# Squares summed while attention runs, a later first weight load, router logits in column groups, the second gate applied on GpSimd, and one block for experts, spare blocks and final sums

## What is computed

```
mods = split(silu(cond) @ w_ada + b, 6)              # shift/scale/gate 1, shift/scale/gate 2
h1   = modulate(rmsnorm(x), shift1, scale1)
f, q, k, v = split(h1 @ w_in)
fout = real(fft2(f, 64 channels x positions)) @ w_fmix
nout = neighbourhood_attention(q, k, v, k_ctx, v_ctx, rpb)   # 12 heads, 8x16 window + 256 context keys
x1   = x + gate1 * (concat(rmsnorm(fout), rmsnorm(nout)) @ w_out)
h2   = modulate(rmsnorm(x1), shift2, scale2)
lg, le = h2 @ w_rg, h2 @ w_re                        # 4 group logits, 32 expert logits
group = argmax(lg);  two experts of the 8 in it;  gate = softmax weight * group probability
y    = sum over the 2 experts of gate * (silu(h2 @ w_gate[e]) * (h2 @ w_up[e])) @ w_down[e]
x2   = x1 + gate2 * y
out  = rmsnorm(x2, g_final)
```

## Time and profile before

| | |
|---|---|
| runs | 1292.05, 1292.8, 1293.32 us, median 1292.8 |
| profiled execution | 1292.83 us, span 1291.0 us |
| busy | PE 1232.0 us (95%), DVE 934.3 (72%), ACT 706.7 (55%), POOL 249.9 (19%) |
| mean granted TensorE clock | 0.981 |
| first tiles | 0 to 34 us |
| projection, attention | 34 to 333, 333 to 518 us |
| mixing, choice and lists | 519 to 640, 640 to 657 us |
| experts | 657 to 1245 us, 17.76 us each |
| finish | 1245 to 1291 us |

### The profile page before, as it was taken

The page is one execution under the profiler, slowest core; times in us unless marked ns, Lnnn a source line. Parts: engine busy times, 40 slices in busy tenths (PEclk is TensorE's granted clock), DMA queues, the critical chain, the costliest instruction groups (busy, mean ns, idle before and its releaser), DMA issues. The chain is left out here.

```text
span 1291.0 us, 18692 instructions
## 1 busy us (share of the span) xinstructions
PE 1232.0 (95%) x7306; PEld 1024.4 (79%) x7306; DVE 934.3 (72%) x1105; ACT 706.7 (55%) x827; POOL 249.9 (19%) x201
## 2 busy tenths in 40 slices
PE   4799999999999999999989999999999999999966
PEld 1799888888788888888878888888888888888852
DVE  2656544332688887556669998989989888989847
ACT  3832212112556665322247777878787877778723
POOL 0000000001101000000011542623535265321001
PEclk8899999999999999999899999999999999999988
DMA  9648844434577772600559999999999999999756
GB/s 379 239 181 295 283 149 157 159 114 164 201 234 160 170 181 81 235 36 34 180 198 354 383 392 390 374 392 376 384 384 377 393 377 390 380 383 386 252 195 262
DMA packets 94459, 343.81 MB, mean 266 GB/s; under 512 B 17387, under 2 KB 45731, under 8 KB 66723
## 3 DMA queue, kind: packets, MB, share of 16 engines
q1 hardware_dynamic: 74499, 311.37, 65.8%
q10 hardware_dynamic: 10656, 14.43, 3.8%
q0 software_dynamic: 9216, 16.80, 3.5%
HBM read 313.70 MB, written 39.33 MB: 273 GB/s over the span
## 5 line engine op out<-in xcount | busy, mean ns | idle before, releaser
L2010 DVE TENSOR_TENSOR w_low<-raw,w_high 128x2048 fp32r<-128x2048 f32 x128 | 293.4, 2313 | 30.8 <-ACT w_high L1950 28.0
L1950 ACT ACTIVATE w_high<-raw 128x2048 fp32r<-128x2048 f32 x128 | 241.1, 1910 | 9.6 <-DVEq L1312 9.6
L2010 DVE TENSOR_TENSOR w_low<-arena,w_high 128x2048 fp32r<-128x2048 f32 x64 | 146.4, 2290 | 31.6 <-ACT w_high L1950 31.6
L1950 ACT ACTIVATE w_high<-arena 128x2048 fp32r<-128x2048 f32 x64 | 122.1, 1908 | 3.2 <-DMA arena<-in_w_down 3.2
L1909 POOL DMA_INDIRECT y_rows<-arena,row x32 | 48.1, 1504 | 324.2 <-ACT arena L1971 322.6
L1867 PE MATMUL p_g<-w_high,x_high 128*128 128x512 f32 x252 | 101.7, 404 | 2.0 <-DVE w_low L2010 1.1
L1867 PE MATMUL p_u<-w_high,x_high 128*128 128x512 f32 x256 | 102.3, 400 | 0.0
L1867 PE MATMUL p_a<-tokens_high,half_high 128*128 128x512 f32 (+1 forms) x272 | 101.8, 374 | 0.2 <-DVE half_low L698 0.2
L1868 PE MATMUL p_a<-tokens_low,half_high 128*128 128x512 f32 (+1 forms) x272 | 100.9, 371 | 0.0
L1869 PE MATMUL p_a<-tokens_high,half_low 128*128 128x512 f32 (+1 forms) x272 | 100.8, 371 | 0.0
L1869 PE MATMUL p_u<-w_high,x_low 128*128 128x512 f32 x256 | 100.0, 391 | 0.0
(11 more groups left out here) (344 smaller groups left out, 2823.4 us busy)
## 6 DMA issues: line engine op xcount, KB each, us to landing
raw<-in_w_gate SPq DMA_DIRECT2D x64, 1024.0 KB, 8.3
raw<-in_w_up SPq DMA_DIRECT2D x64, 1024.0 KB, 7.9
arena<-in_w_down SPq DMA_DIRECT2D x64, 1024.0 KB, 8.4
raw<-in_w_ada SPq DMA_DIRECT2D x24, 1024.0 KB, 7.8
x<-qk_rows SPq DMA_DIRECT2D x6, 1664.0 KB, 9.0
raw<-in_w_chunks SPq DMA_DIRECT2D x9, 1024.0 KB, 5.8
qk_rows<-x SPq DMA_DIRECT2D x18, 512.0 KB, 2.6
yy<-y_rows SPq DMA_DIRECT2D x8, 1024.0 KB, 13.5
```

The lines of the kernel that those rows point to most:

```text
L1950: act.activation(x.high[i % SPLITS][:], x.raw[j][:, :], ACT.Copy).then_inc(high_ok, 1)
L2010: dve.tensor_tensor(x.low[i % SPLITS][:], x.raw[j][:, :], x.high[i % SPLITS][:], ALU.subtract).then_inc(low_ok, 1)
```

## The change

At the start, the first weights are loaded after all eight pieces of `w_ada` instead of after the sixth; only the first half of them is made high in the first block, and all low parts and the second high part move to the projection's start. In attention, the Fourier squares are summed by PE inside steps 8 to 11, the squares of the last pair of tiles move from ACT to DVE (`add_last`), PE sums `acc` between and after the last steps, the eighteen transposes become 4 and 3, and the first tile's high and low parts (`first_high`, `first_low`) are made in steps 43 and 44. The mixing block starts with products. `route` has the weights stationary (64 columns, 36 of them weights, the rest zeros), two halves of k in two column groups, so that the turned logits are copied by ACT (`move_logits`) and joined by one matmul against `pair` (`join`). The last tile's scaling moves to ACT (`scale_last`) and two POOL multiplications and additions. In the experts POOL multiplies each y by gate2 before it is scattered; the last one is multiplied on DVE from PSUM. The finish is in the same block as the experts, starts when all rows are written, and makes each tile of three steps: DVE adds y0 x gate0 (`begin`), ACT multiplies y1 by gate1, POOL adds. Some semaphores and buffers are renamed or shared.

```diff
@@ first_tiles, SP, ACT and DVE
-                    if k == 5:
-                        load_weights(sp, a, s, 0)
+                load_weights(sp, a, s, 0)
-                for q in range(2):
-                    act.activation(half_chunk(s, s.w_high2, q), raw_half(s, q), ACT.Copy).then_inc(s.half_high, 1)
                 act.wait_ge(multiplied, KD)
                 act.activation(flat[0:64, :], p_r[0:64, :], ACT.Copy)
+                wait_weights(act, s, 0)
+                act.activation(half_chunk(s, s.w_high2, 0), raw_half(s, 0), ACT.Copy).then_inc(s.half_high, 1)
-                for q in range(2):
-                    dve.tensor_tensor(half_chunk(s, s.w_low2, q), raw_half(s, q), half_chunk(s, s.w_high2, q), ALU.subtract)
@@ project, ACT and DVE
+                        if g == 0 and r == 0:
+                            split(1)
-                lows(0)
+                for r in range(2):
+                    split(r)
+                    lows(0, (r,))
@@ attention, PE
+                    if NT <= n < NT + NT // 2:
+                        for i in (2 * (n - NT), 2 * (n - NT) + 1):
+                            pe.matmul(s.group_sums[:, NT + i:NT + i + 1], s.f_squares[:, 0, i * P:(i + 1) * P], s.ones[:, 0:1], start=True, stop=True)
@@ mix_and_route, PE
-                    for k in range(KD):
-                        last = pe.matmul(p_l[:, n * 36:(n + 1) * 36], xt[n % 2][:, k, :], wrs[:, k, :], start=(k == 0), stop=(k == KD - 1))
-                    last.then_inc(logits, 1)
+                    for k in range(KD // 2):
+                        for g in range(2):
+                            last = pe.matmul(p_l[64 * g:64 * g + 64, SUMS:SUMS + P], wrs[:, 4 * g + k, :], xt[n % 2][:, 4 * g + k, :],
+                                             start=(k == 0), stop=(k == KD // 2 - 1))
+                    last.then_inc(routed, 1)
+                def join(n):
+                    pe.wait_ge(moved_l, n + 1)
+                    pe.matmul(p_l[:, n * 36:(n + 1) * 36], turned_logits, pair[:], start=True, stop=True).then_inc(logits, 1)
@@ mix_and_route, last tile: ACT, POOL, DVE
+                def scale_last():
+                    act.activation(xrow[(NT - 1) % 2][:], s.x1[:, NT - 1, :], ACT.Copy, scale=rstd[:, 2, NT - 1:NT]).then_inc(scaled_last, 1)
+                pool.tensor_tensor(last[:], last[:], scale2, ALU.mult).then_inc(scaled_last, 1)
+                pool.tensor_tensor(last[:], last[:], shift2, ALU.add).then_inc(scaled_last, 1)
                 halves = one_e.rearrange("p (k n) -> p k n", k=2)
+                dve.wait_ge(scaled_last, 4)
@@ main_experts, POOL
                 pool.wait_ge(y_ok, n + 1)
+                if n < NE - 1:
+                    pool.tensor_tensor(x.y[b], x.y[b], x.gate2[:], ALU.mult).then_inc(y_scaled, 1)
+                    pool.wait_ge(y_scaled, n + 1)
                 pool.indirect_dma_start(a.y_rows, ...
@@ main_experts, DVE, after the last split
+            dve.tensor_tensor(halves(x.y[(NE - 1) % 2]), x.p_y[:], halves(x.gate2[:]), ALU.mult).then_inc(y_ok, 1)
@@ finish (no block of its own)
+        def add(i):                                   # POOL, tiles 0 to 6
+            pool.tensor_tensor(s.x1[:, i, :], s.x1[:, i, :], yy[i][:, 1, :], ALU.add).then_inc(added, 1)
+        def gate(i):                                  # ACT, tiles 0 to 6
+            act.activation(yy[i][:, 1, :], yy[i][:, 1, :], ACT.Copy, scale=s.gates[:, 1, i:i + 1]).then_inc(gated, 1)
+        def begin(i):                                 # DVE, all tiles
+            dve.scalar_tensor_tensor(s.x1[:, i, :], yy[i][:, 0, :], s.gates[:, 0, i:i + 1], s.x1[:, i, :], ALU.mult, ALU.add).then_inc(begun, 1)
+        def end(i):                                   # DVE, tile 7
+            dve.scalar_tensor_tensor(s.x1[:, i, :], yy[i][:, 1, :], s.gates[:, 1, i:i + 1], s.x1[:, i, :], ALU.mult, ALU.add).then_inc(ended, 1)
-NORMS = [(0, 2), (2, 2), (4, 2), (6, 2)]
+NORMS = [(0, 2), (2, 2), (4, 2), (6, 1), (7, 1)]
```

More of the change, by code:

```diff
@@ L1245, in weigh, with sums @@
                     last.then_inc(weighted, 1)
+                def sums(*tiles):
+                    for i in tiles:
+                        pe.matmul(s.group_sums[:, i:i + 1], s.acc[:, i * P:(i + 1) * P], s.ones[:, 0:1], start=True, stop=True)
                 for n in range(STEPS + 2):
@@ L1502, in move_x @@
                     if n >= 2:
[L1503 removed]
+                        dve.wait_ge(routed, n - 1)
                     dve.tensor_copy(xt[n % 2][:, 4:8, :], p_t[1][:].rearrange("p (k q) -> p k q", k=4)).then_inc(t_dve, 1)
[L1506 removed]
+                group_sums()
+                norm_groups()
                 split(EARLY)
[L1508 to L1511 removed]
+                split(EARLY + 1)
                 scale_f(0)
+                split(EARLY + 2)
                 low_f(0)
+                split(EARLY + 3)
                 low(1)
@@ L1653, in _ @@
                 for n in range(NT):
-                    last = pe.matmul(p_r[:, n:n + 1], s.acc[:, n * P:(n + 1) * P], s.ones[:, 0:1], start=True, stop=True)
-                for n in range(NT):
-                    last = pe.matmul(p_r[:, NT + n:NT + n + 1], s.f_squares[:, 0, n * P:(n + 1) * P], s.ones[:, 0:1], start=True, stop=True)
-                last.then_inc(sums_ok, 1)
-                for n in range(NT):
                     mix_na(n)
+                    if n >= 2:
+                        join(n - 2)
                     if n >= 1:
@@ L1999, in _ @@
             split(NE - 1, 5)
-            move_y(NE - 1)
+            act.wait_ge(over_ready, over.STEPS)
+            spare.scalar(act, spare.count(act))
+            last.scalar(act)
         @block.vector
@@ L2049, in _ @@
             split(NE - 1, 5)
+            dve.wait_ge(c_in, 80)
+            dve.wait_ge(scattered[(NE - 1) % 2], 16 * ((NE - 1) // 2))
+            dve.wait_ge(used, place[NE - 1, 5] + 1)
+            halves = lambda y: y.rearrange("p (c n) -> p c n", c=2)
+            dve.tensor_tensor(halves(x.y[(NE - 1) % 2]), x.p_y[:], halves(x.gate2[:]), ALU.mult).then_inc(y_ok, 1)
+            spare.vector(dve, spare.count(dve))
+            last.vector(dve)
         @block.tensor
@@ new lines, in tensor, with body @@
+    def tensor(pe, count):
+        def body(n):
+            pe.wait_ge(q.gathered[0], (n + NE // 2 + 1) * 16)
+            for k in range(KD):
+                last = pe.transpose(x.p_x[:, k, :], every(x.xg[0], k, KD), s.ident[:])
+            last.then_inc(q.x_turned, 1)
+            pe.wait_ge(q.x_high, n + NE + 1)
+            for j in range(4):
+                pe.wait_ge(q.loaded[j], (n + NE + 1) * 16)
+                for i in range(4):
+                    k = 4 * (j % 2) + i
+                    last = pe.matmul((x.p_g, x.p_u)[j // 2][:], x.x_whole[:, k, :], x.raw[j][:, i * DE:(i + 1) * DE],
+                                     start=(k == 0), stop=(k == KD - 1))
+                if j % 2 == 1:
+                    last.then_inc(q.used, 1)
+            pe.wait_ge(q.h_ok, n + NE + 1)
+            for k in range(KE):
+                last = pe.transpose(x.p_h[:, k, :], every(x.h, k, KE), s.ident[:])
+            last.then_inc(q.h_turned, 1)
+            pe.wait_ge(q.h_high, n + NE + 1)
+            for j in (4, 5):
+                pe.wait_ge(q.loaded[j], (n + NE + 1) * 16)
+                for h in range(2):
+                    for i in range(2):
+                        k = 2 * (j - 4) + i
+                        last = pe.matmul(x.p_y[:, h, :], x.h_whole[:, k, :], x.raw[j][:, i * D + h * 512:i * D + (h + 1) * 512],
+                                         start=(k == 0), stop=(k == KE - 1))
+            last.then_inc(q.used, 1)
+        each(pe, count, body)
```

638 lines of the change are left out of this document (339 added, 299 removed).

## The result

The changed kernel takes 1319.6 us (median of 4 runs, 1315.5 to 1322.8) against 1293.1 before: a ratio of 1.019, 95% interval 1.017 to 1.021. I had forecast 1284.4 and faster.

What follows compares the result with a forecast made beforehand. The prediction took TensorE's own work and its waits as the bound (1232.0 of 1291.0 us busy). Terms −1.4 − 2.1 − 1.4 − 3.2 + 1.0 − 0.35 + 2 − 3 = −8.45 took 1292.83 to 1284.4 us, range 1272 to 1299.

Steps and rivals of the forecast that it cites:

- Experts: Expert loop: GpSimd's gate multiplications cost +2 us, mostly covered by VectorE's spare time, with room in GpSimd's queue.
- The price on **VectorE: Experts: GpSimd's multiplication holds VectorE, which has 1.99 us spare per expert; between nothing and +8.6 us, taken as +2.
- Rival A: Experts: each gate multiplication exceeds VectorE's spare time, so VectorE becomes the bound; 1298.9 us or near 1317; chance 0.21.
- second price: Rival A with each multiplication taking 3.0 us from VectorE: +1.0 us per expert, near 1317 us.
- Choice: Expert choice: last tile's scaling on ScalarE and GpSimd slows VectorE's small operations; +1.0 us, up to +2.9.
- Finish: Final sums: earlier loads, additions shared with GpSimd; −3 us, between −8.5 (no disturbance) and +3 (full turns).
- Router and clock: Mixing: cheaper routes by two overlapping column groups, −3.2 us; no clock fall at the first products, −1.4 us.
- Start: Kernel start: later weight load lets the `w_ada` pieces land 2.5 us earlier, 1.1 taken back; −1.4 us.
- End of attention: Attention to mixing: sums moved into earlier steps and fewer transposes bring mixing's first product earlier; −2.1 us.

Runs made afterwards that it cites:

- no_gate: Changed kernel with GpSimd's 31 gate multiplications left out of the experts: 1291.5 us, ratio 0.998.
- spread: Changed kernel with GpSimd's 80 small table operations issued 3 or 4 at a time in experts 1 to 24 instead of in bunches: 1292.6 us, ratio 0.999.
- places_spread: Changed kernel with only the two bunches of eight 128x128 table operations spread, two in each of experts 17 to 24: 1301.3 us, ratio 1.005.
- spread_finish_dve: The kernel of spread, with VectorE making both sums of every tile in the finish, none on GpSimd, no gate scaling on ScalarE: 1286.0 us, ratio 0.993.
- route_old: Changed kernel with VectorE replacing GpSimd for gate, last tile's scaling and finish sums, plus the earlier kernel's router: 1284.2 us, ratio 0.993.
- start_old: Changed kernel with VectorE replacing GpSimd for gate, last tile's scaling and finish sums, plus the earlier kernel's start: 1283.2 us, ratio 0.992.
- gate_any: Changed kernel multiplying by x1 of tile 0 instead of the gate rows, which are loaded only in the last expert: 1320.1 us, ratio 1.020.
- before_gate: Kernel before the change, plus GpSimd multiplying each of the first 31 results by x1 of tile 0 before its scatter: 1308.2 us, ratio 1.013.

## Why the prediction was wrong

The step that failed is in **Experts**: "POOL is nearly empty ... the queue behind (a gather, needed an expert later) can stand 2.4 us". I read it from GpSimd's 19% of the span and from an expert without tables. In five of the eight experts with a bunch GpSimd was still at work on it, or on the gather behind it, when the next result was ready to be scattered, and the gather behind the bunch landed only 1.4 to 4.3 us before its use. (In the other three it had 3.6 to 5.6 us of rest.) Four of these five gathers are the ones that TensorE waits for in the changed kernel. I had L1825 in the earlier trace rows as evidence on VectorE, with its 4.72 us, and didn't add eight of them up against the next gather. The runs show the size: against no_gate, the same multiplications cost 28 us (changed kernel) or 1.1 (spread), by where the table operations stand. places_spread gives 18 of the 27 us between the changed kernel and spread to the two bunches of L1935. The lower clock behind the late gathers, 4.6 us in the trace, is a term that the prediction's experts did not have at all.

The price on **VectorE** was nearly right. The hold is 2.2 us (I had bounds of 0 and 2.37), that is 0.2 above the 1.99 of spare time, by the prediction's own sum 30 × 0.2 − 2.8, some 3 us, and the stretch of spread is 542.3 against 540.9 before: +1.4 for my +2. Rival A, VectorE as the bound of all experts, happened only with the doubled multiplication. Its second price, near 1317, lies close to the measured 1319.6 by accident: it has every period 1.0 us longer, and 16 of the 31 in the changed kernel are within 0.1 of the 17.76 of before. The Trainium skill (SBUF — State Buffer, section "SBUF: two separate sides") has this as an exclusive lock for a whole instruction; the traces agree, 4.50 for 2.28 beside a multiplication of 2.37, and 6.75 for 2.48 beside two additions. By that page's rule the prediction had +8.6 for this term, where spread shows +1.4, and 1298.9 with the choice and the finish: slower, but for another reason than the one that decided.

**Choice**: right mechanism, mis-sized. The prediction's upper bound was +2.9 and the stage grew by 4.4. Two of VectorE's small operations lost 3.7 us, and the traces with and without GpSimd's two operations are 3.6 apart on average.

**Finish**: I took the middle between no collision (−8.5) and full turns (+3), reasoning that the scalings fall where GpSimd is free (the terms of the −8.5 give an end at 1279.0, not 1279.4). They don't: it is +2.8 from the last product. spread_finish_dve gives back 6.3 us of the finish although it adds seven VectorE operations.

**Router and clock**: −3.2 − 1.4 forecast, −5.6 measured; a route costs 1.02, and the clock does not fall at the first products. route_old, which has the old router and the new end of attention, splits it: its mixing takes 115.8 us with a granted clock of 1.00 up to 630.7, against 117.2 before, so some 1.4 is the clock, as forecast. The router is 2.5 us by the medians, 4.5 by one pair of traces, some 3.4 where the clock falls at the stage's end in both. **Start**: −1.4 forecast, −0.8 in the first pair of traces, −1.7 in start_old's. **End of attention**: −2.1 forecast, −1.2 in the first pair. The stage from the first score takes 186.4 to 188.9 us in traces with the new code and 188.6 and 190.2 in the two with the old, so its size is not resolved. The sum itself has a slip: the terms between the last weighing and the first product add up to 1.9, not 2.3.

One thing stays partly open: why the changed kernel and gate_any lose some 10 us more than before_gate, with the same multiplications and the same bunches. It is neither the gate rows nor the wait for them. The traces say where it lies. The stretch is 21.8, 26.8 and 10.7 us longer than before in the three; the waits for gathers are 14.0, 22.7 and 8.6 of it, and the lower clock behind them 4.6, 4.2 and 1.7. So it lies in how late a few gathers are, the longest wait being 8.1, 8.5 and 2.8. Why they are so much later is not shown. The runs of one kind lie up to 10 us apart (1315.5 to 1322.8, 1314.8 to 1324.5, and 1307.5 to 1314.9), and the second bunch of eight, ahead of the last of these gathers, took 17.7 us in before_gate and 21.8 in the changed kernel. That a late gather shifts this to the worse and so feeds itself is plausible and was only argued.

## What to carry to other kernels

An engine's busy share over the span says nothing about its fullest stretch. Before adding work to an engine that issues transfers, find the transfer with the least time between landing and use, list what stands ahead of it in that queue, and add the new work there. In all three places here work on GpSimd was paid for on VectorE too. In the finish, seven operations of 1.28 us more on VectorE were cheaper than seven additions of 2.37 on GpSimd. And when added work proves dear, try its neighbours' places in the queue before its removal: order alone gave back 27 us here. When TensorE has to wait for several microseconds, look at the granted clock behind the wait as well: it added a third to the price of the waits here.

## What the runs showed of the hardware

In a wait of 8.13 us the granted clock fell to 0.50 and stayed there for the first 6 us of TensorE's work behind it. A scatter's descriptor work on GpSimd took 1.50 us before and 2.25 in most experts of the changed kernel, at its new place behind the multiplication. GpSimd's side of a meeting also stretches: the multiplication takes 2.37 alone and 3.14 on average in the experts (2.37 to 4.51), and eight operations of 128x128, which can take 0.60 each, took 17.3 to 21.8 us together. Eight fp32 matmuls with 64 stationary and 128 moving columns, in two column groups in turn, pass in 1.02 us, where eight with 128 stationary and 36 moving columns took 1.70.
